# Index keys gathered with dimensions on the partitions, by 128 small transfers; index scores turned on TensorE instead of sent through DRAM

## What is computed

```python
def indexer_scores(qi, wi, ki):
    s = jnp.einsum('bqhd,bld->bqhl', qi, ki).astype(jnp.float32) * IDX_DIM ** -0.5
    return jnp.einsum('bqhl,bqh->bql', jax.nn.relu(s), wi.astype(jnp.float32)) * IDX_HEADS ** -0.5
...
    ki_past = cik[page_table].reshape(db, past, IDX_DIM)
    ki_all = jnp.concatenate([ki_past, ki_new.astype(ki_past.dtype)], axis=1)
    idx, valid = select_topk(indexer_scores(qi, wi, ki_all), q_pos, k_pos, topk)
```

## Time and profile before

| what | value |
|---|---|
| median of three runs | 1301.05 us (1296.62 to 1303.74) |
| profiled execution | 1301.76 us, its span 1300.0 us |
| PE busy | 1259.1 us (97%) |
| DVE busy | 698.3 us (54%) |
| ACT busy | 466.6 us (36%) |
| POOL busy | 188.0 us (14%) |
| granted TensorE clock, mean | 0.985 of full |

### The profile page before, as it was taken

One profiled execution on the slowest core, in us unless ns is written; L12 is line 12 of the kernel. 1 busy time (PEld: TensorE's weight loads), 2 busy tenths in 40 slices (PEclk: granted clock), 3 DMA queues, 4 the chain that ended last, 5 costly groups with the idle time before them and its releaser, 6 DMA issues.

```text
span 1300.0 us, 24718 instructions
## 1 busy us (share of the span) xinstructions
PE 1259.1 (97%) x10122; PEld 1217.7 (94%) x10122; DVE 698.3 (54%) x1290; ACT 466.6 (36%) x541; POOL 188.0 (14%) x281
## 2 busy tenths in 40 slices
PE   5999998889999999999999999999999999999997
PEld 5979995577999999999999999999999999999996
DVE  5468997775365555555322254546655555552322
ACT  5242336652143433434222243334333434332110
POOL 1001002135041111111000010033111111110000
PEclk9999999998989999999999999999999999999998
DMA  6664302023022222222222332121222222222211
GB/s 220 170 119 146 114 34 80 1 100 98 1 105 96 97 97 97 87 77 95 90 90 89 105 126 98 66 99 65 98 97 97 76 85 97 97 89 90 90 63 66
DMA packets 26595, 120.40 MB, mean 93 GB/s; under 512 B 7880, under 2 KB 9224, under 8 KB 14504
## 3 DMA queue, kind: packets, MB, share of 16 engines
q1 hardware_dynamic: 21784, 107.67, 24.6%
q0 software_dynamic: 2048, 10.54, 2.4%
q10 hardware_dynamic: 2704, 1.35, 0.4%
HBM read 115.94 MB, written 3.61 MB: 92 GB/s over the span
## 4 chain that ended last, share of the span: by engine, by line
PE 70%; DVE 2%; ACT 0%; issue 0%; DVEq 0%
PE ps L880 22%; PE ps L881 22%; PE ps L883 22%; PE ps L1016 1%; PE ps L1013 1%; PE ps L1014 1%; PE ps L899 1%; PE ps L1366 1%; DVE vtc L2022 0%; DVE yt L2069 0%; DVE xn L1423 0%; PE ps L1383 0%; PE ps L1356 0%; PE ps L1396 0%; DVE w_l L1409 0%; DVE ut L2015 0%
## 5 line engine op out<-in xcount | busy, mean ns | idle before, releaser
L880 PE MATMUL ps<-xh,w_h 128*128 128x260 f32 x1664 | 435.5, 283 | 0.2
L881 PE MATMUL ps<-xl,w_h 128*128 128x260 f32 x1664 | 434.3, 282 | 0.0
L883 PE MATMUL ps<-xh,w_l 128*128 128x260 f32 x1664 | 334.1, 282 | 0.0
L880 PEld LDWEIGHTS ps<-xh,w_h 128*128 128x128 f32 x1664 | 313.6, 188 | 0.7 <-DVE res L1824 0.3
L881 PEld LDWEIGHTS ps<-xl,w_h 128*128 128x128 f32 x1664 | 312.9, 188 | 0.1
L1409 DVE TENSOR_TENSOR w_l<-w_raw,w_h 128x2048 fp32r<-128x2048 f32 (+1 forms) x94 | 213.0, 2266 | 158.7 <-ACT w_h L526 158.5
L883 PEld LDWEIGHTS ps<-xh,w_l 128*128 128x128 f32 x1664 | 256.1, 188 | 0.0
L526 ACT ACTIVATE w_h<-w_raw 128x2048 fp32r<-128x2048 f32 (+1 forms) x50 | 92.3, 1845 | 256.4 <-PE ps L883 209.3
L881 PE MATMUL ps<-hl,w_h 128*128 128x260 f32 x704 | 183.9, 282 | 0.0
L880 PE MATMUL ps<-hh,w_h 128*128 128x260 f32 x704 | 183.4, 282 | 0.0
L883 PE MATMUL ps<-hh,w_l 128*128 128x260 f32 x704 | 141.8, 283 | 0.0
(11 more groups left out here) (323 smaller groups left out, 1575.7 us busy)
## 6 DMA issues: line engine op xcount, KB each, us to landing
w_raw<-in_wstream SPq DMA_DIRECT2D x86, 1024.0 KB, 4.8
w_raw<-in_wstream SPq DMA_DIRECT2D x8, 768.0 KB, 4.7
res<-in_x_t SPq DMA_DIRECT2D x4, 520.0 KB, 7.1
out_y<-yt SPq DMA_DIRECT2D x8, 260.0 KB, 2.2
tab<-bias_by_distance SPq DMA_DIRECT2D x16, 128.0 KB
wor<-in_wstream SPq DMA_DIRECT2D x4, 512.0 KB, 6.2
wm<-in_sgu_w ACTq DMA_DIRECT2D x1, 512.0 KB, 3.7
sb_b<-in_sgu_b ACTq DMA_DIRECT2D x1, 512.0 KB, 4.4
```

The lines of the kernel that those rows point to most:

```text
L880: pe.matmul(out[h], wh, hi[h], start=(first and k == 0), stop=False)
L881: pe.matmul(out[h], wh, lo[h], start=False, stop=False)
L883: ins = pe.matmul(out[h], wl, hi[h], start=False, stop=(last and k == nk - 1))
```

## The change

The host lays the index cache out as (page, dimension, token), so a row is one dimension of one page's 128 tokens (512 bytes). A gather of 128 such rows gives 2 pages x 64 dimensions on the partitions by 128 tokens: a block that PE can take as it is. A sample is 16 such gathers, all samples 128, into five buffers instead of two (`IK_BUF`; three of them lie over tiles that are free at that time). The turns, their copies on ACT and `ikt` are gone. The table of rows (`rows`, 128x128) is worked out ahead of the sums of squares instead of in group 0. POOL's list has the gathers between its other work. The bias table's 16 transfers (`tab`) move on SP from the fifth slab to behind the ninth, as their place is used by two of the buffers. The scores are laid as (2, sample, 16), and at the end of group 9 PE turns them with three transposes into PSUM, from which `key_halves` reads; the two trips to DRAM and POOL's mask are gone. `score` has one more small reduction.

```diff
-                if s == 5:
+                if s == 9:
                     sp.wait_ge(d_scr, 32)
+                    sp.wait_ge(sc_unit, 16)
...
-            sp.wait_ge(sc_all, 2)
-            sp.dma_start(bass.AP(by_token.ap().tensor, 0, [[NT, P], [NT * P, DEC], [1, NT]]), sc[:]).then_inc(d_bytok, 16)
...
-                act.activation(flat(ikt[u % 4][:]), ps[:, 4 + u % 2, :], ACT.Copy).then_inc(ev_a, 1)
...
-                for q in range(4):
-                    ins = pe.transpose(ps[:, bank, q * P:(q + 1) * P], ik[b % 2][:, (c0 + q) * P:(c0 + q + 1) * P], ident[:])
-                ins.then_inc(tr_done, 1)
...
+                if u % 4 == 0:
+                    pe.wait_ge(s_ik[IK_BUF[b]], 256 * (IK_USE[b] + 1))
...
-                    ins = pe.matmul(ps[:, 6 + b % 2, c:c + 16], ikt[u % 4][:, q, :], qibd[:, b, :], start=True, stop=True)
+                    ins = pe.matmul(ps[:, 6 + b % 2, c:c + 16], ik[IK_BUF[b]][:, 4 * (u % 4) + q, :], qibd[:, b, :], start=True, stop=True)
...
+            def turn_scores():
+                pe.wait_ge(col_new, 1)
+                for t in range(2):
+                    pe.transpose(ps[:, 7, t * P:(t + 1) * P], sc[:, t].rearrange("p b c -> p (b c)"), ident[:])
...
+            def gather(b, parts):
+                for i in parts:
+                    c = 16 * b + i
+                    pool.indirect_dma_start(out=ik[IK_BUF[b]][:, i, :], out_offset=None, in_=cache_i,
+                                            in_offset=bass.IndirectOffsetOnAxis(ap=rows[:, c:c + 1], axis=0))\
+                        .then_inc(s_ik[IK_BUF[b]], 16)
```

More of the change, by code:

```diff
@@ L160, in build_step @@
         o_ik = o
-        ik = [at(f"ik{i}", [P, RUN * 64], F32, o + 8192 * i) for i in range(2)]; o += 16384
-        sc = at("sc", [P, DEC, NT], F32, o)
+        ik_home = (o_ik, o_ik + 8192, o_h, o_h + 8192, o_tmp)
+        ik = [at(f"ik{i}", [P, 16, P], F32, ik_home[i]) for i in range(5)]; o += 16384
+        sc = at("sc", [P, 2, DEC, 16], F32, o)
+        new_col = at("new_col", [P, DEC, 16], F32, o + 1024)
         pp = at("pp", [P, 2, NK], F32, o); o += 2112
@@ L182, in build_step @@
         wax = at("wax", [P, 2, 4, P], F32, o_qi)
-        ikt = [at(f"ikt{i}", [P, 4, P], F32, o_tmp + 2048 * i) for i in range(4)]
+        pt = at("pt", [P, P], I32, o_gg + 6720)
+        rows = at("rows", [P, P], I32, o_relu + 7488)
         kv = at("kv", [P, 4, 4, 2 * P], F32, o_ik)
@@ L309, in build_step @@
         rows_done, prep, wib_rhs, wib_mm = sem("rows_done"), sem("sample_prep"), sem("wib_rhs"), sem("wib_mm")
-        s_ik = [sem(f"ik_landed{i}") for i in range(2)]
-        tr_done, ev_a = sem("tr_done"), sem("ev_a")
+        s_ik = [sem(f"ik_landed{i}") for i in range(5)]
         sc_mm, sc_free, sc_all = sem("sc_mm"), sem("sc_free"), sem("sc_all")
@@ L418, in _ @@
                 sp.dma_start(dst[:], src).then_inc(done, 16)
+            sp.dma_start(pt[:], pages).then_inc(d_pt, 16)
             load(1, 1)
-            for dst, src, done in ((pt, pages, d_pt), (pg2, page2, d_const),
+            for dst, src, done in ((pg2, page2, d_const),
                                    (blocks, c_blocks, d_const), (picks, c_pick, d_const), (h0s, h0, d_rgs)):
@@ L611, in _ @@
                         split(10, 0)
-                    piece = sample_piece(g, step)
-                    if piece and piece[1] in (0, 2, 4, 6):
-                        evac_unit(4 * piece[0] + piece[1] // 2)
             gelu_a(9)
@@ L1433, in _ @@
                     ALU.subtract).then_inc(x_lo, 1)
+            dve.wait_ge(d_pt, 16)
+            ts(rows[:], pt[:], 64.0, col("row_in_page", 0), ALU.mult, ALU.add).then_inc(rows_done, 1)
+            ch.link(dve.memset(new_col[:], OUT))
             for g in range(1, 4):
@@ L1593, in _ @@
                     norm_scale(0)
-                    dve.wait_ge(d_pt, 16)
-                    ts(rows[:], pt[:], 4.0, col("row_mod4", 0), ALU.mult, ALU.add).then_inc(rows_done, 1)
                 if g == 3:
@@ L1625, in _ @@
                             last = score(b)
+                            if b == DEC - 1:
+                                last.then_inc(col_new, 1)
                 if g == 9:
@@ L1635, in _ @@
                     q += rounds[g][2]
-            last.then_inc(sc_all, 1)
             dve.wait_ge(a_free, 10)
             dve.wait_ge(b_free, 10)
-            dve.memset(sc2[:, 2 * P:NK], OUT).then_inc(col_new, 1)
             dve.memset(zero1, 0.0)
@@ L2092, in _ @@
             pool.tensor_copy(beforeb[:], blocks[:, 1, :]).then_inc(blocks_b, 1)
+            pool.memset(qibd[:], 0.0).then_inc(d_bef0, 1)
+            pool.wait_ge(rows_done, 1)
+            gather(0, range(16))
+            gather(1, range(16))
+            pool.wait_ge(stat_mm, 1)
+            gather(2, range(6))
+            later_columns(1)
+            gather(2, range(6, 16))
+            later_columns(2)
+            gather(3, range(8))
+            later_columns(3)
+            pool.wait_ge(prep, 1)
+            pool.wait_ge(idx_mm, 24)
+            pool.memset(wax[:], 0.0).then_inc(wax0, 1)
+            gather(3, range(8, 16))
+            pool.wait_ge(wi_nat, 1)
+            gather(4, range(16))
             for j in range(4):
@@ L2095, in _ @@
                     .then_inc(d_rgc, 16)
[L2096 to L2111 removed]
+            for b in (5, 6):
+                pool.wait_ge(sc_unit, 4 * (b - 4))
+                gather(b, range(16))
             pool.wait_ge(a_free, 8)
```

86 lines of the change are left out of this document (25 added, 61 removed).

## The result

The changed kernel takes 1316.8 us (median, 1316.7 to 1321.2) against 1301.1 beside it: 1.0112 of the time before, interval 1.0088 to 1.0137. It is slower, as forecast, by 15.7 us where 20 were named. Its profiled execution took 1316.8 us with a span of 1315.1, so it stands for the median; the span before was 1300.0.

The account below looks back on a forecast made before the run. PE, 97% busy, was taken to bound the kernel, with POOL's gathers making it wait after the change. The sum: 1301.8 + 19.9 - 0 = 1321.7 us, 1321 against the median; range 1307 to 1333.

Parts of the forecast that it names:

- the likeliest case: Whole kernel: slower by about 20 us, 1321 against the median, 1313 to 1330 by its terms; chance 0.55.
- The gather's price: POOL's 128 gathers: 0.95 us each plus 0.30 of issue, by rows not bytes; period 1.25, together 160.0 us.
- Hold-ups: POOL's gathers beside DVE's two-input operations: nine splits lose 14.0 us, sums of squares 3.2; together 17.2 (0 to 23.7).
- the second rival: The convolution's and accumulation's two-input operations hold gathers too: 3.5 to 4 us, 1325; with late landings 1333; chance 0.19.
- Which wait decides: Group 9: PE begins at 194 behind POOL's copies and DVE's convolution, waits for sample 7 until 203.9; last evacuation 218.5.
- Half clock: PE in group 9, behind the longer stalls: granted clock falls to 1.2 GHz, costing 1.7 us.
- Sample 5's stall: Early in group 8: PE stands some 14 us, until sample 5 lands at 162; covered by the later stall.
- The bias table: Its transfers move on SP behind PE's 16th unit (about 137 us); needed only after 209, so 0.
- PE's gain capped at 5 us by DVE: Input projection: 14.1 us of PE's turns removed, but DVE's room allows 5 us if POOL kept up (0 to 9).
- The DRAM trip: Scores' trip before DVE's first count: the 1.0 us saved is given back waiting for PE; 0 (bounds 0 and 1.0).
- The rival without hold-ups: POOL's train: DVE doesn't hold up gathers, so POOL ends 12.8 us earlier; 1308, chance 0.12.
- the one in which POOL keeps up: POOL's gathers come at less than 1.16 us, PE gives back its turns up to DVE's room: 1296, faster; chance 0.10.

Follow-up runs that it names:

- the run with the states early: The changed kernel with POOL's copies of the conv states ahead of sample 6's gathers instead of behind them: 1328.0 us, ratio 1.0162.
- the two kernels that take the gathers off the path: The changed kernel with every second gather left out: 1298.5 us, 0.9963; the kernel before without PE's turns and ACT's copies: 1298.9 us, 0.9963.

## Why the prediction was right, and where its terms were off

The direction, its mechanism and its size were right: POOL's issue of the gathers, and what stands behind them on POOL, sets the end, and 1316.8 lies in the narrower range of the likeliest case. By its steps:

- **The gather's price**, 0.95 + 0.30 us by rows and not by bytes: 0.944 + 0.30. Right. The whole train ran from 16.85 to 197.1 us; I had 16.7 to 200.4.
- **Hold-ups**, 17.2 us: 15.1. Eight gathers were caught by a split and lost 1.46 us each on the mean (1.55 taken); the ninth split fell on the conv states' transfers. The three gathers beside the sums of squares lost 1.0 (3.2 taken: I had counted three operations of 1.3 us as one of 3.9). The operations of the second rival do hold gathers up, and so far the rule of the Trainium skill that it quoted holds, but the four caught beside the convolution lost 0.3 each, 1.3 in all against the 2 estimated, and those beside the accumulation 0.8 in all against another 2.
- **Which wait decides.** I had the convolution at 179.5 and PE's start of group 9 at 194, and then a further wait for sample 7, landed at 203.9. The first came at 176.1 and the second at 191.8. The further wait was not there: at half clock PE reached sample 7 only at 199.4, and the gather issued by 197.1 had landed in 2.4 us or less, not the 4.7 of the later train. So the path is POOL's first 112 gathers, the state copies, the convolution, group 9. Group 9 took 21.4 us from its start, 4.3 of them the clock's, so 17.1 at full clock; the forecast had 24.5, with 1.7 for the clock and so 5.7 of waiting that did not come. (It named 6.9, from 197 to 203.9; but it had left out sample 6's last unit and new token, 1.2 us that PE does ahead of sample 7.) This is the step that failed: it set the end by sample 7 instead of by the copies. The two lie close together, as the run with the states early shows.
- **Half clock**, 1.7 us: 4.3. I had carried over the price behind a 1.3 us stall to one of 8.4. With the start 2.2 us earlier, 5.7 us of waiting gone and 2.6 us of clock more, 218.5 becomes 213.2, as measured. That two of these errors go against each other, so that the forecast is 5 us off and not 8, is luck.
- **Sample 5's stall**, 14 us, to 162: 13.0 us, to 160.0. Right, and hidden as said. Sample 6 I had at 182, some 10 us behind PE by 10.4 us a sample; it was 1.65 us, to 176.8, since PE at half clock needed 15 us from one to the other and the last gather had landed 1.6 us or less after its issue. Hidden as well.
- **The bias table**, 0: wrong as a step, harmless in the sum. I asked only when the table is needed, not what its 2 MB do to the gathers under way. It held sample 5 back by 4 us or more, hidden under the state copies' wait; moved, it made PE wait 10.7 us for sample 6 or 13.7 for sample 7.
- **PE's gain capped at 5 us by DVE** (0 to 9): 4.8 to 5.2 us by the two kernels that take the gathers off the path, 6 at the evacuation. An evacuation moved forward gives 2.4 us more there; that the rest stays with DVE's busy time and the clock is argued, not shown.
- **The DRAM trip**, 0: 10.49 us from the last evacuation to the first count in both kernels, with 2.76 us of waiting for PE in place of 1.95 and the 1.0 for DRAM. Right. The second reduction took 0.15 us, as estimated.

The rival without hold-ups and the one in which POOL keeps up are excluded by the rows on the gathers.

## What to carry to other kernels

An indirect gather is paid by the issue on its engine, not by its bytes: before one large gather is cut into many small ones to save another engine's work, multiply the count by the period (here 1.25 us) and compare it with the whole stage; then look at what else stands in that engine's queue, for it was a copy of 0.8 us behind the gathers that stopped everything, and with the copy moved ahead it was the last gathers themselves. What removed work is worth is read from the next engine's order: 14 us of matrix work gave 5, and one evacuation moved forward made room for 2 more at the end of the stage. And a transfer has two due times, its own and those of the transfers that are under way beside it.

## What the runs showed of the hardware

- A one-input `tensor_scalar` of 2048 elements that runs at 0.60 ns an element held a gather that began inside it as the two-input form did; in both the gather ended 0.8 us after the DVE operation. Unlike the two-input form it also held five gathers that had begun 0.1 to 0.5 us ahead of it, until 0.1 us after its end.
- Transfers that SP issues with the address in a register cost its queue 0.80 us each (51.5 us for 64, the loads of the page numbers included), and 1.05 us behind the table.
- The 2 MB of the table, cut into 16 transfers of 128 KB on SP's queue, slowed gathers of POOL's queue from 2.4 us or less to some 11 between issue and landing, at a DMA share of only 0.54 to 0.57 in the windows of 170 to 190.
- PE's clock was at half after stalls of 8 to 16 us, for 5 to 20 us, and once after one of 2.5 us, for 10 us. It also dips in the later stages of every one of these kernels at times of its own, which moved the rest of the program between 1101 and 1108 us: enough to hide a gain of 4 us.
